# Expert down projection: the 48-row block in plain fp32 on two column halves, raw down weights in two buffers, rows fetched ahead of stores

## What is computed

```python
combine = ...                       # top group, then the top 2 experts inside it
for e in range(N_EXPERTS):          # 16
    h = jax.nn.silu(t @ w_gate[e]) * (t @ w_up[e])     # 1024 -> 256
    y = y + combine[:, e:e + 1] * (h @ w_down[e])      # 256 -> 1024
x = layer_norm(DEEPNORM_ALPHA * x + y, ln_moe_g, ln_moe_b)
```

## Time and profile before

| | |
|---|---|
| median of 3 runs | 984.9 us (980.77 to 986.08) |
| the profiled execution | 989.0 us, of which the span is 987.2 us |
| PE busy, share of the span | 951.2 us, 96% |
| DVE, ACT, POOL busy | 592.8, 350.8, 196.8 us |
| granted TensorE clock, mean | 0.986 |
| first gate/up matmul of the experts | at 704.5 us |

### The profile page before, as it was taken

One profiled execution on the slowest core, in us unless ns is written; L12 is line 12 of the kernel. 1 busy time (PEld: TensorE's weight loads), 2 busy tenths in 40 slices (PEclk: granted clock), 3 DMA queues, 4 the chain that ended last, 5 costly groups with the idle time before them and its releaser, 6 DMA issues. The chain is left out here.

```text
span 987.2 us, 15735 instructions
## 1 busy us (share of the span) xinstructions
PE 951.2 (96%) x5687; PEld 805.0 (82%) x5687; DVE 592.8 (60%) x1279; ACT 350.8 (36%) x737; POOL 196.8 (20%) x256
## 2 busy tenths in 40 slices
PE   7999999999999999999999999999999999999995
PEld 6899888677767888788877888889879888888984
DVE  6744341487676776655575554567534476767676
ACT  6123031243376555410024333231232344444342
POOL 0012100121142220012220000004300134343435
PEclk9999999899999999999999999998999999999998
DMA  9122010000699500620116000044788888989872
GB/s 310 56 86 86 1 65 1 1 1 1 234 414 395 182 24 22 211 109 1 52 38 211 3 1 1 1 171 166 266 272 291 270 302 278 314 303 328 305 277 94
DMA packets 67278, 151.60 MB, mean 154 GB/s; under 512 B 8720, under 2 KB 16144, under 8 KB 67216
## 3 DMA queue, kind: packets, MB, share of 16 engines
q1 hardware_dynamic: 59920, 133.82, 38.9%
q0 software_dynamic: 7296, 16.95, 4.5%
HBM read 107.62 MB, written 52.03 MB: 162 GB/s over the span
## 5 line engine op out<-in xcount | busy, mean ns | idle before, releaser
L1970 PEld LDWEIGHTS h_ps<-xgT,e_gate_up 128*128 128x128 f32 x1024 | 155.6, 192 | 4.5 <-issue 2.2
L1970 PE MATMUL h_ps<-xgT,e_gate_up 128*128 128x176 f32 x1024 | 157.1, 315 | 2.2 <-DVEq L2078 2.2
L262 PE MATMUL unit_ps<-whi,xhi 128*128 128x512 f32 (+1 forms) x256 | 98.1, 383 | 6.2 <-DVE wlo L294 6.2
L263 PE MATMUL unit_ps<-wlo,xhi 128*128 128x512 f32 (+1 forms) x256 | 98.0, 383 | 0.0
L264 PE MATMUL unit_ps<-whi,xlo 128*128 128x512 f32 (+1 forms) x256 | 97.9, 383 | 0.0
L262 PEld LDWEIGHTS unit_ps<-whi,xhi 128*128 128x128 f32 x256 | 48.7, 190 | 14.0 <-DVE xlo L338 6.2
L2113 DVE SCALAR_TENSOR_TENSOR z<-y_ps,slot_weight,x_rows 128x512 f32<-128x512 f32 (+1 forms) x64 | 45.6, 746 | 23.7 <-PE y_ps L1984 21.0
L264 PEld LDWEIGHTS unit_ps<-whi,xlo 128*128 128x128 f32 x256 | 48.6, 190 | 7.8
L263 PEld LDWEIGHTS unit_ps<-wlo,xhi 128*128 128x128 f32 x256 | 48.6, 190 | 7.5
L1982 PE MATMUL y_ps<-e_dn_hi,h_hi 128*128 128x512 f32 (+1 forms) x128 | 52.1, 407 | 1.2 <-DVE z L2113 1.1
L1984 PE MATMUL y_ps<-e_dn_hi,h_lo 128*128 128x512 f32 (+1 forms) x128 | 50.2, 392 | 0.0
(11 more groups left out here) (342 smaller groups left out, 2167.9 us busy)
## 6 DMA issues: line engine op xcount, KB each, us to landing
e_gate_up<-w_gu SPq DMA_DIRECT2D x16, 2048.0 KB, 10.7
e_down_raw<-w_dn SPq DMA_DIRECT2D x16, 1024.0 KB, 5.3
slot_rows<-zeros SPq DMA_DIRECT2D x22, 522.0 KB, 6.3
slot_sums<-zeros SPq DMA_DIRECT2D x22, 512.0 KB, 6.3
x_rows<-slot_rows SPq DMA_DIRECT2D x16, 522.0 KB, 4.5
slot_sums<-z SPq DMA_DIRECT2D x16, 512.0 KB, 4.4
wraw<-w_in SPq DMA_DIRECT2D x24, 256.0 KB, 4.6
xraw<-xT SPq DMA_DIRECT2D x16, 256.0 KB, 5.0
```

The costliest lines, as they stand in the source:

```text
L262: pe.matmul(o, hi, whi[:, s, 0:w], start=(s == 0), stop=False)
L263: pe.matmul(o, hi, wlo[:, s, 0:w], start=False, stop=False)
L1970: end = pe.matmul(hps[:, m, gu * CAP:(gu + 1) * CAP], gate_up[:, b, s, w], xT[:, s, :], start=(s == 0), stop=(s == KD - 1))
```

## The change

1. Units 2 and 3 (the 48-row block) are computed by plain fp32 products from `h` and the raw weights: 4 products of 512 columns in place of 12. Unit 2 writes partitions 0 to 47 and unit 3 partitions 64 to 111 of the same bank, and the two are issued in turn. One increment of `ysum` by 2 follows both. `h_hi` and `h_lo` shrink from 176 to 128 columns.
2. The raw down weights have two buffers. The load for step e+2 is issued at the end of step e on SP, after the last down product; that for expert 1 is issued before the steps.
3. SP issues the rows of a block (two steps ahead) as soon as that block's evictions are done, ahead of that block's store.
4. `BANK` becomes `[0, 1, 2, 2]`; PE waits for evictions of the step before only, never for one of its own step.

```diff
+    gate_up, dn_raw = k.e_gu, [k.e_dn, at("e_down_raw_odd", 150, [P, 4, 512])]
+    SMALL = slice(P, CAP)
-    hhi = at("h_hi", 146, [P, 2, CAP], f32r)
-    hlo = at("h_lo", 147.5, [P, 2, CAP], f32r)
+    hhi = at("h_hi", 146, [P, 2, P], f32r)
+    hlo = at("h_lo", 147.5, [P, 2, P], f32r)
-    BANK = [0, 1, 2, 0]
+    BANK = [0, 1, 2, 2]
+    FROM = [0, 0, 0, 64]
@@ sync
+            sp.dma_start(dn_raw[1][:], A["w_dn"][1].rearrange("s p n -> p s n")).then_inc(dn_loaded[1], 16)
             def step(n, h, g_, e, b):
-                last = is_one_of_last(e, 1)
-                if not last:
-                    hold(dn_lo_done, n(4, 4))
-                    sp.dma_start(dn_raw[:], A["w_dn"][bass.ds(n(1, 1), 1)].rearrange("a s p n -> p (a s) n")).then_inc(dn_loaded, 16)
                 if not is_one_of_last(e, 2):
                     hold(gsum, n(2, 2))
                     sp.dma_start(gate_up[:, b], A["w_gu"][bass.ds(n(1, 2), 1)].rearrange("a s p n -> p (a s) n")).then_inc(gu_loaded[b], 16)
                 hold(z_stored, n(32, 128))
+                hold(placed_at, n(1, 1))
                 for c in range(2):
                     hold(z_made, n(4, 2 * c + 6))
+                    if not is_one_of_last(e, 2):
+                        fetch(n(CAP, 2 * CAP), b, [c])
                     sp.dma_start(k.z_dram[bass.ds(n(CAP, c * P), ROWS[c]), :], z[c][:]).then_inc(z_stored, 16)
                 if not is_one_of_last(e, 2):
-                    hold(placed_at, n(1, 1))
-                    fetch(n(CAP, 2 * CAP), b)
+                    hold(ysum, n(4, 12))
+                    sp.dma_start(dn_raw[b][:], A["w_dn"][bass.ds(n(1, 2), 1)].rearrange("a s p n -> p (a s) n")).then_inc(dn_loaded[b], 16)
@@ tensor (down(j, f) keeps the three fp32r products, for the 128-row block alone)
-                for u, free in ((0, 4), (1, 2), (2, 3)):
-                    pe.wait_ge(z_made, n(4, free))
-                    down(u, 0)
+                for j in range(2):
+                    pe.wait_ge(z_made, n(4, j + 1))
+                    down(j, 0)
                 pe.wait_ge(hlo_done, n(2, 2))
-                for u in range(3):
-                    down(u, 1).then_inc(ysum, 1)
-                pe.wait_ge(z_made, n(4, 5))
-                down(3, 0)
-                down(3, 1).then_inc(ysum, 1)
+                for j in range(2):
+                    down(j, 1).then_inc(ysum, 1)
+                pe.wait_ge(z_made, n(4, 4))
+                for f in range(2):
+                    for u in (2, 3):
+                        j = UNITS[u][1]
+                        end = pe.matmul(yps[FROM[u]:FROM[u] + B1, BANK[u], :], hh[:, f, SMALL], dn_raw[b][:, 2 * f + j, :], start=(f == 0), stop=(f == 1))
+                end.then_inc(ysum, 2)
@@ scalar
-                    act.activation(hhi[:, m, :], hh[:, m, :], ACT.Copy).then_inc(hhi_done, 1)
+                    act.activation(hhi[:, m, :], hh[:, m, 0:P], ACT.Copy).then_inc(hhi_done, 1)
-                    act.wait_ge(dn_loaded, n(16, 32))
+                    act.wait_ge(dn_loaded[1 - b], h(16, 16 * (1 + b)))
@@ vector
-                    dve.tensor_tensor(hlo[:, m, :], hh[:, m, :], hhi[:, m, :].bitcast(f32), ALU.subtract).then_inc(hlo_done, 1)
+                    dve.tensor_tensor(hlo[:, m, :], hh[:, m, 0:P], hhi[:, m, :].bitcast(f32), ALU.subtract).then_inc(hlo_done, 1)
-                    dve.scalar_tensor_tensor(z[c][:, f], yps[r, BANK[u], :], wgt[r, b, c:c + 1], rows[b][r, c, f], ALU.mult, ALU.add,
+                    dve.scalar_tensor_tensor(z[c][:, f], yps[FROM[u]:FROM[u] + ROWS[c], BANK[u], :], wgt[r, b, c:c + 1], rows[b][r, c, f], ALU.mult, ALU.add,
```

More of the change, by code:

```diff
@@ L1290, in _ @@
             sp.wait_ge(w_lo, XH)
-            sp.dma_start(k.e_dn[:], A["w_dn"][0].rearrange("s p n -> p s n")).then_inc(k.dn_loaded, 16)
+            sp.dma_start(k.e_dn[:], A["w_dn"][0].rearrange("s p n -> p s n")).then_inc(k.dn_loaded[0], 16)
             sp.dma_start(k.g3[:], over(A["ln_moe_g"], [P, D])).then_inc(k.gains_loaded, 16)
@@ L1775, in experts @@
     g, b_ = k.g3, k.b3
-    gate_up, dn_raw = k.e_gu, k.e_dn
+    gate_up, dn_raw = k.e_gu, [k.e_dn, at("e_down_raw_odd", 150, [P, 4, 512])]
+    SMALL = slice(P, CAP)
     xT = k.xgT
@@ L1842, in hold, with fetch @@
                 sp.sem_inc(held_sp, 1)
-            def fetch(row, b):
-                for c in range(2):
+            def fetch(row, b, blocks=range(2)):
+                for c in blocks:
                     sp.dma_start(rows[b][0:ROWS[c], c, :], k.xs_dram[bass.ds(row + c * P, ROWS[c]), :]).then_inc(rows_loaded[b], 16)
@@ L1975, in step, with down @@
                     turn(1 - b, h(32, 32 * (1 + b)))
-                def down(u, f):
-                    c, j = UNITS[u]
+                def down(j, f):
                     w = 2 * f + j
-                    hi, lo = (t[:, f, c * P:c * P + ROWS[c]] for t in (hhi, hlo))
-                    out = yps[0:ROWS[c], BANK[u], :]
+                    hi, lo, out = hhi[:, f, :], hlo[:, f, :], yps[:, j, :]
                     pe.matmul(out, hi, dn_hi[:, b, w, :], start=(f == 0), stop=False)
@@ L2009, in split_down @@
                 for s in range(4):
-                    act.activation(dn_hi[:, b, s, :], dn_raw[:, s, :], ACT.Copy).then_inc(dn_hi_done, 1)
+                    act.activation(dn_hi[:, b, s, :], dn_raw[b][:, s, :], ACT.Copy).then_inc(dn_hi_done, 1)
             act.sem_inc(ysum, 8)
             act.wait_ge(stats_cleared, 6)
-            act.wait_ge(dn_loaded, 16)
+            act.wait_ge(dn_loaded[0], 16)
             split_down(0)
@@ L2047, in split_down @@
                     dve.wait_ge(dn_hi_done, n(4, s + 1))
-                    dve.tensor_tensor(dn_lo[:, b, s, :], dn_raw[:, s, :], dn_hi[:, b, s, :].bitcast(f32), ALU.subtract).then_inc(dn_lo_done, 1)
+                    dve.tensor_tensor(dn_lo[:, b, s, :], dn_raw[b][:, s, :], dn_hi[:, b, s, :].bitcast(f32), ALU.subtract).then_inc(dn_lo_done, 1)
             def know_high(e, b):
@@ L2345, in program @@
     k.e_dn = at("e_down_raw", 89, [P, 4, 512])
-    k.gu_loaded, k.dn_loaded = [k.sem("gate_up_loaded_even"), k.sem("gate_up_loaded_odd")], k.sem("down_loaded")
+    k.gu_loaded, k.dn_loaded = [k.sem("gate_up_loaded_even"), k.sem("gate_up_loaded_odd")], [k.sem("down_loaded_even"), k.sem("down_loaded_odd")]
     k.g3, k.b3 = at("ln3_g", 97, [P, D]), at("ln3_b", 101, [P, D])
```

## The result

| | kernel before | kernel after |
|---|---|---|
| median of 11 runs each | 983.07 us (979.87 to 986.08) | 987.68 us (978.84 to 991.84) |
| ratio after to before | | 1.0049, 95% interval 1.0027 to 1.007 |
| profiled execution's span | 987.2 us | 982.4 us (its own time 984.18) |
| granted TensorE clock, mean | 0.986 | 0.990 |
| first gate/up to the end | 282.7 us | 284.7 us |

The change makes the kernel slower, by 0.5%, where 1% faster was forecast. The two profiled spans alone would say the opposite, and the last row of the table says why: the profile of before reached the experts at 704.49 us and that of after at 697.67. That stage isn't touched by the change, and in the profiles of this study it ended anywhere from 697.5 to 704.5.

The account below looks back on a forecast made before the run. PE was taken to set the time, but barely, with POOL's ring and the DMA engines close. 12.4 us gained, less 1.5 for the ring and 1.0 for DMA, is 9.9: 984.9 to 975.0 us, range 971 to 982.5.

Parts of the forecast that it names:

- the change on PE: Down products on PE: 2.75 us removed, 1.72 and 0.2 added, so -0.83 us per step and a period of 15.92.
- Rival C: The two column halves on PE run one after the other, +0.88 us per step, 997 us; chance 0.07.
- D: Rival on PE: streams overlap but weight loads stand between them, +0.14 us per step, near 986 us; chance 0.03.
- POOL's ring: POOL's loop over stores, landing wait and `put_out` wants 16.0 to 16.3 us against 15.92; 1.5 us lost, bounds 0 and 7.
- landing wait of 8.0: Upper bound for POOL's wait from second store to next copy: ring 17.0 us, giving the loss bound of 7 us.
- The step that failed: DVE's 2.97 us idle before the second `h` hides POOL's lateness; only what exceeds it stalls PE.
- a gain to be had: PE's wait for bank 0 in two long steps, behind late gathers, goes: 1.5 us back, 1.4 taken.
- Rival B: POOL's ring or the DMA engines take over, steps 5 to 13 stay near 17 us; 980.5 us, chance 0.20.
- the 0.6 predicted: Last step: both halves of block 1 come together after the last matmul, adding 0.6 us to the tail.
- The change on SP: Block 1 rows issued near 6.4 us land at 13.1, needed at 14.2; without the reordering late in a bad step.
- The 1.0 us for DMA throughput: Late steps hold 16.1 us of DMA work, which doesn't fit into 15.92; 1.0 us lost, bounds 0 and 3.
- Rival E: The change doesn't reach the time: late rows or a late down load eat all of it and more; 981 to 992, chance 0.04.

Follow-up runs that it names:

- experiment 4: Changed kernel with unit 3 writing partitions 0 to 47 of bank 0, so both halves share the same 64 columns; 1016.53 us, ratio 1.0314.
- experiment 8: Changed kernel with SP issuing the 2 MB gate/up load only once that step's gathers have landed, from step 4 on; 989.09 us, ratio 1.0047.
- experiment 7: Changed kernel with the down load in the steps' loop cut to 16 columns of 512; 983.97 us, ratio 0.9999.
- experiment 3: Changed kernel without POOL's low-sum gathers and DVE's wait for them; 974.79 us, ratio 0.9902.
- experiment 9: Changed kernel with POOL's wait for the landing of the out stores moved behind the next gathers; 970.21 us, ratio 0.9845.
- experiments 1 and 11: 1: new down products, SP's order of the kernel before, two raw buffers, ratio 1.0084; 11: the same with POOL's landing wait behind the next gathers, ratio 0.9976.
- experiment 12: Changed kernel with 64 already met waits behind PE's last step, ahead of its last branch; 981.49 us, ratio 0.9986.

## Why the prediction was wrong

**Right: the change on PE.** Down 4.80 us (4.78 predicted), the four products 1.93 with the first gap, the early period 16.05 (15.92). The missing 0.1 is in the gate/up block: from its start to the transposes 9.65 us for 9.55, the only part of the step that grew. Rival C is out (experiment 4 shows what the stretch would have been, 3.63 us), and so is D: the loads, 0.12 us each, cost nothing between streams of 0.43. The Trainium skill (TensorE: Matmul & The Clock Gate, Part 3, What overlaps and what doesn't) says that a weight load overlaps running matmuls only when its row group differs, which would make D true here; these rows don't agree with it.

**Right in kind, short in size: POOL's ring.** The forecast had `put_out` late by 0.6 once, then by 0.4 a step. It was late by 0.7 in step 6, 1.6 in step 7, and up to 3.7. From step 6 to step 7 it slid by 0.97 in a period of 16.05, so the ring took 17.0 there: POOL's next copy started 7.97 us after the second store, which is the landing wait of 8.0 that the forecast had as its bound, in place of the 7.3 taken.

**The step that failed** is the one behind it: "PE doesn't see it at once: DVE has 2.97 us idle before the second `h`, and only what exceeds that stalls PE." The slack was taken from one consumer of POOL's work, `put_out`. POOL's list has another, the gathers, and their slack was far less. At a lateness near 1 us they fall in with or behind the 2 MB gate/up load and land 6 to 7.5 us after issue, where most second gathers of before took 3.1 to 4.0 (experiment 8 takes the load away, and in steps 6 to 10 they land in 2.3 to 4.5). This adds some 3 us at one stroke, to the first eviction and all that SP has queued behind it, and feeds back into POOL. The rows showed it: two late gathers in the kernel before, with 2.6 us of waits, were booked as a gain to be had and not as a warning. Rival B was discounted because gathers would no longer meet the down load; experiment 7 all but removes that load, and they are late still. What stalled PE in the late steps was not the second `h` but the rows for its transposes (4.3 us in four steps; the fifth wait in the list above is in the first step), and the late steps cost 5.5 us together. How much of this is the slow landing and how much POOL's own lateness isn't shown: experiment 3 takes both away, experiment 9 moves the gathers early, and in experiment 8, with quick landings, another wait of the same size came up.

**The end was left out.** Lateness was priced by what it does to the steps; but the last step has no next one to hide it in. What POOL is behind when the last `put_out` comes is paid there in full, and with it a clock at 0.50: 5.8 us of tail for the 0.6 predicted. With no lateness (experiment 9) the last step takes 17.75 for 17.47, so the change itself is worth 0.3 of it.

**Not foreseen:** 3.0 us in the last branch on PE.

**The change on SP** was judged rightly: it is needed (experiments 1 and 11). The 1.0 us for DMA throughput was too much when nothing else is late (experiment 9 shows 0). Rival E, at a chance of 0.04, names what came (late rows eat all of it and more, 981 to 992), without a mechanism for the late rows. Rival B, the nearest in kind, named POOL's ring but put its price at 980.5, since it had neither the gathers nor the end in it. With the measured terms the sum is 12.4, less 1.8 for the period (0.70 for 0.83, 14 times), less 5.5 for late steps, 5.2 for the tail and 3.0 for the branch, and 1.0 more by the first period and the way to the last down: -2.1, as the traces have it. The range reached no further than 982.5 because it was built on the one slack.

**Open:** why two or three steps of a run collide and others not, which makes the runs of after scatter; how much lead a gather needs (see the last section: with 1.0 us most land quickly and some don't); and the rest of the difference of the medians, 2.6 us above what the profiles show.

## What to carry to other kernels

When the engine that sets the pace gets faster, list everything the second-slowest ring feeds, and take the slack of the consumer with the least of it; here that was a transfer that just got ahead of a large load, and the loss of 1 us of lead cost it about 3. Lateness that is hidden inside a loop is paid in full in the last turn. Where a wait for a landing sits in front of independent work, move it behind that work together with the faster part: here neither alone gained, and both gave 1.5%.

## What the hardware showed that was not expected

- Two streams of plain fp32 products into different 64-column halves overlap whether issued in turn or four records of one after four of the other: 1.93 us for 8 records both ways, 3.63 in one half.
- All profiles together, steps 6 and later, gathers whose issue on POOL wasn't stretched: issued up to 3.5 us behind the 2 MB load they took 5.9 to 8.1 us to land, in each of 37 cases. Issued 0.3 to 0.9 us ahead of it they took anything from 2.2 to 7.4. Issued 0.9 to 1.1 us ahead they took 2.3 to 4.7 in 13 cases of 15, and 6.0 and 6.1 in the other two. With no such load near, in the last two steps of after, it was 3.1 to 4.3.
- PE's last branch takes 0.4 or 3.4 to 3.9 us. 64 more instructions ahead of it took it from the one to the other (experiment 12). What decides it inside the chip wasn't looked into.
- POOL's instructions that fall beside DVE's split are stretched: a gather's issue 3.45 us for 1.14, a copy of two columns 3.65 for 0.18, both in after.
